# Two-block transformer kernel: MLP up products with both activation parts as one 512-column operand, scale applied after the down products, four transfers moved in the load queue

## Chip, cores and metric

The kernel runs on one core of one Trainium2 chip. The metric is the device time of one execution in microseconds. The kernel before was timed three times; the median is 1084.58 us (1083.57 to 1085.78).

## The reference, cut to what matters

A sequence of 256 tokens with 1024 channels goes through two transformer layers and then through a second block. Three MLPs of the same form lie on the way, each with 4096 hidden channels, all in float32:

```python
def rmsnorm(x, g):
    return x * rsqrt(mean(x * x, -1) + EPS) * g
def sq_relu_mlp(h, w_up, w_down):
    u = relu(h @ w_up)
    return (u * u) @ w_down
x = x + sq_relu_mlp(rmsnorm(x, g_mlp), w_up, w_down)     # MLP 0 and MLP 1, first block
x = x + square(relu(rmsnorm_2(x, g2) @ w_ff1)) @ w_ff2   # MLP 2, second block
```

Around them stand a gated linear attention, a sliding-window attention, and in the second block a mixer with an input projection of 5888 columns, a full attention of 8 heads, a dilated attention of 12 heads and gates.

## The kernel before, in words

**Products.** TensorE works on float32 values in a reduced format (fp32r). To keep precision, every operand stands as a high part (rounded to fp32r) and a low part (the rest), and a product is three matmuls: high x high, high x low, low x high (`prod`, L269). In `gemm_a` (L284) the weights are the stationary operand (128 x 128) and the transposed activations hT move, 256 columns (all tokens) per matmul, so the order of one product is weight-high with hT-high, weight-high with hT-low, weight-low with hT-high: three matmuls and three weight loads. In the down products and `gemm_b` the activations are stationary and 512 columns of weights move.

**Weights.** They come in 161 blocks of 1 MB at most (2048 floats per partition). Numbered from 0, blocks 17 to 48 are MLP 0, 58 to 89 MLP 1, 90 to 112 the second input projection (of which 105 to 108 are gate a and 109 to 112 gate b), 113 to 116 the output projection of the full attention, 117 and 118 that of the dilated one, 119 to 122 `w_out_2` ("po"), 123 to 154 MLP 2, 155 to 160 the end. A block is loaded into one of three raw buffers, ACT rounds it into one of three high buffers (`highs_to`, L1674), and DVE subtracts to get the low part (`lows_to`, L932), in two instructions of 1024 columns per block. At the start of block i (`take`), ACT makes the high part of block i+2, which waits for its transfer and for PE's last use of block i-1; DVE makes the low part of block i+1. All engines work in program order, so what stands behind such a wait waits too.

**The load queue.** All loads are issued by SyncE in one order written by hand (`sync_program`, L2252). `weights_to(n)` issues all blocks below n; block j waits for the low part of block j-3, which frees its raw buffer. Between these calls stand small loads that wait for their destination to come free, and hold up every block behind them: the two halves of the gate bias (L2315, which waits for the last transposed head to be read out, and L2317, which waits for the end of the dilated attention), the input p_2 (L2319, waits for the last head of the full attention) and the last norm's gain (L2321, waits for the transposes of p).

**An MLP** (`mlp`, L406 on PE, L1055 on DVE, L1768 on ACT) has 16 up tiles of 256 hidden channels and 16 down blocks, in eight chunks of two and two. The up tiles of chunk c+1 come before the down blocks of chunk c. An up tile is one PSUM bank: i = 0, 1 (128 channels each) times eight k, so 16 products. Four PSUM banks (4 to 7) are taken in turn for it, by the transposes and by small products; banks 0 to 3 hold the sum of the down products. When an up tile is full:

1. DVE writes r = max(tile, 0) times RB, the reciprocal root of the norm, with the row of tokens along the free dimension (L1063). RB comes from a matmul of ones with a diagonal matrix (`rows_scale`, L374 on PE, L1020 on DVE, and `diagonals`, L1013), which can only be made after the sum of squares, DVE and POOL work beside the first tiles. So tiles 0 and 1 are both read out after tile 1.
2. ACT squares r in place (L1776) and rounds it into the high part of u (L1779).
3. DVE subtracts and gets the low part of u (L1070).

At the start of an MLP the first tile is cut in two halves over k; between them PE transposes the second half of x (`norm_rest`, L367), ACT rounds it and DVE makes its low part (L1724, L985), and PE goes on. ACT's high part of the third block of the MLP stands ahead of these roundings in ACT's order. At the end DVE adds the four down sums to x (`add_x`, L1038).

The lines that decide the order of an up tile on DVE:

```python
        def fill(n):                                     # L1058
            for w in due(K.full(tile), m_free, *rb(s)):
                dve.wait_ge(*w)
            stt(r, K.bank(tile), 0.0, RB[:, :], ALU.max, ALU.mult).then_inc(*K.emptied(tile))
        def down_chunk():                                # L1086
            for kk in range(2):
                take()
                u_lows()
```

## Time and profile before

| | before |
|---|---|
| median of three runs | 1084.58 us |
| the profiled execution's own time | 1084.3 us |
| its span in the profile | 1082.5 us |
| TensorE clock granted, mean | 0.98 |
| PE matmul busy | 1023.6 us (95%) |
| weight loads busy (beside the matmuls) | 895.3 us (83%) |
| DVE busy | 647.5 us (60%) |
| ACT busy | 491.1 us (45%) |
| weights read by the load queue | 180.16 MB |

The span runs from the first to the last instruction; the time of an execution is 1.8 us longer. Busy time of PE says that the engine had a matmul under way, not that it ran at its peak: matmuls overlap, and what one costs is read from the starts of consecutive ones.

### The profile page before, as it was taken

The numbers are of one execution on the slowest core, as the hardware profiler recorded it, in microseconds if no ns is written. First come the engines' busy times: TensorE is split into PE (matmuls) and PEld (weight loads), VectorE is DVE, ScalarE is ACT, GpSimd is POOL, SyncE is SP. The second block draws the span as 40 slices with busy tenths as digits, with TensorE's granted clock in tenths as the row PEclk, the third lists the DMA queues.
The fourth block names the chain that finished last, engine by engine and source line by source line (L and its number), as shares of the span: only waits on it lengthen the run. The fifth ranks groups of instructions, "written<-read, shape, count | busy, mean of one in ns | idle before, by whom it ended". The sixth has DMA issues, their size and how long they took to land.

```text
span 1082.5 us, 14500 instructions
## 1 busy us (share of the span) xinstructions
PE 1023.6 (95%) x6158; PEld 895.3 (83%) x6158; DVE 647.5 (60%) x909; ACT 491.1 (45%) x573; POOL 43.2 (4%) x57
## 2 busy tenths in 40 slices
PE   6989999999999879999999999899999799999996
PEld 5866789999989768999989889778777699999975
DVE  4665766555456876645554756675666565455564
ACT  4353445444435654534444464243564344444452
POOL 1000100000000000000000111300000000000001
PEclk8989999999999999999999999899999899999999
DMA  7772475556653326655566465231336446646541
GB/s 216 254 242 78 152 237 195 161 190 200 213 183 106 117 78 200 229 184 161 190 202 210 133 207 182 93 122 35 141 127 214 156 132 216 197 156 194 176 165 49
DMA packets 115033, 181.09 MB, mean 167 GB/s; under 512 B 4351, under 2 KB 78567, under 8 KB 114968
## 3 DMA queue, kind: packets, MB, share of 16 engines
q1 hardware_dynamic: 114968, 180.16, 50.5%
q8 instruction: 48, 0.79, 0.3%
q14 instruction: 17, 0.14, 0.0%
HBM read 179.05 MB, written 5.55 MB: 171 GB/s over the span
## 4 chain that ended last, share of the span: by engine, by line
PE 84%; DVE 6%; DMA 4%; ACT 2%; POOL 2%; issue 1%; SPq 0%; DVEq 0%; POOLq 0%; ACTq 0%
PE ps L263 81%; PE ps L267 3%; DMA raw<-in_a_w_in 2%; DVE wlo L916 2%; DVE M L924 1%; DVE M L916 1%; POOL st L2161 1%; DMA raw<-in_w_ff 1%; ACT whi L1666 1%; ACT RR L1666 1%; DMA raw<-in_w_in 1%; POOL M L2161 0%; ACT M L1663 0%; DVE M L920 0%; DMA x<-in_x 0%
## 5 line engine op out<-in xcount | busy, mean ns | idle before, releaser
L263 PE MATMUL ps<-whi,RR 128*128 128x512 f32 (+2 forms) x1568 | 495.8, 391 | 9.4 <-DVE wlo L916 5.7
L1666 ACT ACTIVATE whi<-raw 128x2048 fp32r<-128x2048 f32 (+1 forms) x161 | 302.3, 1880 | 232.4 <-PE ps L263 201.1
L916 DVE TENSOR_TENSOR wlo<-raw,whi 128x1024 fp32r<-128x1024 f32 (+1 forms) x322 | 372.5, 1200 | 55.4 <-ACT whi L1666 55.2
L263 PE MATMUL ps<-RR,whi 128*128 128x256 f32 (+1 forms) x2016 | 371.1, 286 | 17.6 <-DVE RR L924 12.3
L263 PEld LDWEIGHTS ps<-whi,RR 128*128 128x128 f32 x1568 | 295.2, 190 | 73.8 <-issue 10.0
L263 PEld LDWEIGHTS ps<-RR,whi 128*128 128x128 f32 (+1 forms) x2016 | 318.5, 193 | 23.7 <-DVE RR L924 13.3
L263 PE MATMUL ps<-wlo,RR 128*128 128x512 f32 (+2 forms) x784 | 304.3, 388 | 0.0
L263 PE MATMUL ps<-RR,wlo 128*128 128x256 f32 (+1 forms) x1008 | 287.0, 285 | 0.0
L263 PEld LDWEIGHTS ps<-RR,wlo 128*128 128x128 f32 (+1 forms) x1008 | 194.6, 193 | 0.2
L263 PEld LDWEIGHTS ps<-wlo,RR 128*128 128x128 f32 x784 | 149.1, 190 | 27.7
L924 DVE SCALAR_TENSOR_TENSOR M<-ps,RB 128x512 f32<-128x512 f32 x52 | 35.7, 691 | 177.0 <-PE ps L263 176.2
L1663 ACT ACTIVATE M<-M 128x512 f32<-128x512 f32 (+3 forms) x58 | 41.8, 727 | 159.7 <-DVE M L924 159.4
L263 PE MATMUL ps<-M 128*64 128x128 f32 (+5 forms) x416 | 67.6, 337 | 6.1 <-ACT M L1666 3.2
L263 PEld LDWEIGHTS ps<-M 128*64 128x64 f32 (+2 forms) x416 | 47.2, 164 | 23.4 <-issue 13.5
L1666 ACT ACTIVATE M<-ps 128x512 f32<-128x512 f32 (+2 forms) x49 | 28.4, 597 | 72.9 <-PE ps L267 37.4
L2158 POOL TENSOR_SCALAR st<-st 128x2 f32<-128x2 f32 (+3 forms) x13 | 7.7, 595 | 907.8 <-DVE st L1007 640.5
L267 PE MATMUL ps<-ident,M 128*128 128x128 f32 (+1 forms) x194 | 28.5, 283 | 14.6 <-DVE M L920 6.3
L267 PEld LDWEIGHTS ps<-ident,M 128*128 128x128 f32 (+1 forms) x194 | 22.3, 144 | 22.2 <-issue 14.6
L1666 ACT ACTIVATE RR<-ps,G 128x256 fp32r<-128x256 f32 x64 | 25.1, 480 | 32.3 <-PE ps L267 32.3
L924 DVE SCALAR_TENSOR_TENSOR RR<-ps,G,RR 128x256 fp32r<-128x256 f32 x64 | 26.4, 477 | 21.0 <-ACT RR L1666 21.0
L916 DVE TENSOR_TENSOR x<-x,ps 128x512 f32<-128x512 f32 x24 | 16.5, 686 | 30.3 <-PE ps L263 30.3
L916 DVE TENSOR_TENSOR RR<-M,RR 128x512 fp32r<-128x512 f32 x48 | 32.6, 685 | 0.0
(87 smaller groups left out, 394.0 us busy)
## 6 DMA issues: line engine op xcount, KB each, us to landing
raw<-in_w_up SPq DMA_DIRECT2D x32, 1024.0 KB, 5.4
raw<-in_w_down SPq DMA_DIRECT2D x32, 1024.0 KB, 5.0
raw<-in_w_ff SPq DMA_DIRECT2D x32, 1024.0 KB, 5.4
raw<-in_w_in SPq DMA_DIRECT2D x23, 1024.0 KB, 5.3
raw<-in_a_w_in SPq DMA_DIRECT2D x12, 1024.0 KB, 7.5
raw<-in_a_w_out SPq DMA_DIRECT2D x4, 1024.0 KB, 5.3
raw<-in_b_w_q SPq DMA_DIRECT2D x4, 1024.0 KB, 5.2
raw<-in_b_w_out SPq DMA_DIRECT2D x4, 1024.0 KB, 5.0
```

The lines of the kernel that those rows point to most:

```text
L263: return pe.matmul(out, lhsT, rhs, start=start, stop=stop, skip_group_check=True)
L267: return pe.transpose(out, in_, ident[0:n, 0:n])
L916: return dve.tensor_tensor(out, a, b, op)
L924: return dve.scalar_tensor_tensor(out=out, in0=a, scalar=s, in1=b, op0=op0, op1=op1)
L1663: return act.activation(out, in_, f, **k)
L1666: return act.activation(out, in_, ACT.Copy, **k)
L2158: return pool.tensor_scalar(out, a, s1, s2, op0, op1)
L2161: return pool.tensor_tensor(out, a, b, op)
```

## The change

In the up products of the three MLPs hT's high and low parts, which lie one after the other in the same tensor, become one moving operand of 2 x 256 columns. A product is then two matmuls: weight-high with both parts (512 columns into a whole PSUM bank), and weight-low with hT-high (256 columns, added onto the second half of the bank). A tile of two such banks holds two unfinished sums side by side, and takes a pair of banks. ACT copies the second halves to SBUF, DVE adds the first halves, then DVE computes max(r, 0) * r from SBUF in one instruction; ACT rounds the result, DVE subtracts, as before. RB, the diagonal and the rows matmul are gone from the MLPs: since the square of relu(c x) is c squared times that of x, for c above 0, the square of the norm factor is applied per token (per partition) when the down sums are added to x. POOL computes it (`squared` in place of `eighth`). In the load queue the four small loads each stand two weight blocks later.

```diff
--- before.py
+++ after.py
@@ -140,6 +140,8 @@
                     RR[:, a + 2048:a + 4096].rearrange("p (k t) -> p k t", t=T))
         self.hT, self.yT = parts(0), parts(4096)
+        self.hT2 = RR[:, 0:4096].rearrange("p (a k t) -> p k a t", a=2, t=T)
         self.uT = [(RR[:, 4096 + 2048 * i:5120 + 2048 * i].rearrange("p (k t) -> p k t", t=T),
                     RR[:, 5120 + 2048 * i:6144 + 2048 * i].rearrange("p (k t) -> p k t", t=T)) for i in range(2)]
         self.oB = (RR[:, 8192:8704].rearrange("p (k t) -> p k t", t=T),
@@ -313,6 +315,36 @@
                 after(f)
             yield
+    def gemm_up(name, w, c0, n, ready, hook=None):
+        for f in range(0, n, 256):
+            j, hi, lo = block(w[:, c0 + f:c0 + f + 256], 8, 256)
+            tile = name + (f,)
+            take(tile, *misc_pair())
+            b = K.pair(tile, 512)
+            for w_ in due(K.at("w_lo", j)):
+                pe.wait_ge(*w_)
+            halves = [(0, 4), (4, 8)] if hook and f == 0 else [(0, 8)]
+            for k0, k1 in halves:
+                for i in range(2):
+                    for k in range(k0, k1):
+                        for w_ in due(ready(k)):
+                            pe.wait_ge(*w_)
+                        mm(b[:, i, :].rearrange("p (a t) -> p a t", a=2), hi[:, k, 128 * i:128 * i + 128],
+                           V.hT2[:, k, :, :], k == 0, False)
+                        t = mm(b[:, i, T:2 * T], lo[:, k, 128 * i:128 * i + 128], hT[0][:, k, :], False, k == 7)
+                    if i == 0 and len(halves) == 1:
+                        yield
+                if len(halves) == 2 and k0 == 0:
+                    at = turn["misc"]
+                    hook()
+                    turn["misc"] = at
+                    yield
+            t.then_inc(*K.filled(tile))
+            K.value["w_used", j] = K.full(tile)
+            yield
     def gemm_b(name, w, c0, n, xT, ready, pairs=None):
         kt = xT[0].shape[1]
@@ -405,16 +437,9 @@
     def mlp(l, up, down, s, after):
         ready = h_ready(s)
-        seen = {"n": 0}
-        def scaled(f):
-            seen["n"] += 1
-            if seen["n"] == 2:
-                rows_scale(s)
         def up_chunk(c4):
-            return gemm_a(("up", l, 2 * c4), up, c4 * 512, 512, hT, ready,
-                          (lambda: norm_rest(s)) if c4 == 0 else None, scaled)
+            return gemm_up(("up", l, 2 * c4), up, c4 * 512, 512, ready, (lambda: norm_rest(s)) if c4 == 0 else None)
         dn = {}
@@ -1041,6 +1066,13 @@
             dve.wait_ge(*w)
         tt(xc, xc, K.bank(tile), ALU.add).then_inc(*K.emptied(tile))
+    def add_scaled(tile, n, c, s):
+        xc = x[:, c, n * 512:n * 512 + 512]
+        for w in due(K.full(tile), K.at("rstd2", s)):
+            dve.wait_ge(*w)
+        stt(xc, K.bank(tile), st[:, 6 + c:7 + c], xc, ALU.mult, ALU.add).then_inc(*K.emptied(tile))
     def project(name, s, hook):
         g = gemm_b(D, 8, lambda f, m, c: add_x((name, f, c), f // 512, c))
         next(g)
@@ -1052,15 +1084,19 @@
-    def mlp(l, s, after, m_free):
+    def mlp(l, s, after):
         state = {"n": 0, "late": []}
         def fill(n):
             tile = ("up", l, n // 2 * 2, n % 2 * 256)
             r = V.up_r(n)
-            for w in due(K.full(tile), m_free, *rb(s)):
-                dve.wait_ge(*w)
-            stt(r, K.bank(tile), 0.0, RB[:, :], ALU.max, ALU.mult).then_inc(*K.emptied(tile))
+            r2 = r.rearrange("p (i t) -> p i t", i=2)
+            for w in due(K.at("up_low", (l, n))):
+                dve.wait_ge(*w)
+            tt(r2, r2, K.pair(tile, T), ALU.add).then_inc(*K.emptied(tile))
+            for w in due(K.empty(tile)):
+                dve.wait_ge(*w)
+            stt(r, r, 0.0, r, ALU.max, ALU.mult).then_inc(*K.up("up_u", (l, n)))
             state["late"].append(n)
         def u_lows():
@@ -1073,14 +1109,7 @@
         def evac(f):
             n = state["n"]
             state["n"] += 1
-            if n == 0:
-                diagonals(s)
-                return
-            if n == 1:
-                rows_scale(s)
-                fill(0)
-            else:
-                u_lows()
+            u_lows()
             fill(n)
         def down_chunk():
@@ -1094,7 +1123,7 @@
             for n, c in ((0, 0), (0, 1), (1, 0), (1, 1)):
                 if (n, c) == (1, 1):
                     norm_early(after)
-                add_x(("dn", l, n, c), n, c)
+                add_scaled(("dn", l, n, c), n, c, s)
         g = gemm_a(512, evac, lambda: norm_rest(s))
         next(g)
@@ -1307,7 +1336,7 @@
     gated(1)
     project("pa", 1, lambda: turn_parts("to", 1, None))
-    mlp(0, 1, 2, K.full(("to", 1, 1)))
+    mlp(0, 1, 2)
@@ -1404,7 +1433,7 @@
     next(attn)
     run_all((project_by_rows(), 1), (attn, 1))
-    mlp(1, 3, 4, K.empty(("pr", 1, 1)))
+    mlp(1, 3, 4)
@@ -1618,7 +1647,7 @@
     tt(pT[1].rearrange("p k t -> p (k t)"), K.bank(("pT",)), pT[0].rearrange("p k t -> p (k t)").bitcast(F32),
        ALU.subtract).then_inc(*K.emptied(("pT",)))
-    mlp(2, 5, 6, K.full(("ty", 1, 1)))
+    mlp(2, 5, 6)
@@ -1765,27 +1794,23 @@
-    def mlp(l, s, after, u_free):
+    def mlp(l, s, after, m_free, u_free):
         state = {"n": 0}
         def fill(n):
             tile = ("up", l, n // 2 * 2, n % 2 * 256)
             r = V.up_r(n)
-            for w in due(K.empty(tile)):
+            low = K.pair(tile, 512)[:, :, T:2 * T]
+            for w in due(K.full(tile), m_free, *([K.at("u_lo", (l, n - 4))] if n >= 4 else [])):
                 act.wait_ge(*w)
-            d = step(actf(r, r, ACT.Square))
-            for w in due(d, *(u_free if n < 4 else [K.at("u_free", (l, n // 2 - 2))])):
+            copy(r.rearrange("p (i t) -> p i t", i=2), low).then_inc(*K.up("up_low", (l, n)))
+            for w in due(K.at("up_u", (l, n)), *(u_free if n < 4 else [K.at("u_free", (l, n // 2 - 2))])):
                 act.wait_ge(*w)
             copy(V.u_part(n, 0), r).then_inc(*K.up("u_hi", (l, n)))
         def evac(f):
-            n = state["n"]
+            fill(state["n"])
             state["n"] += 1
-            if n == 0:
-                return
-            if n == 1:
-                fill(0)
-            fill(n)
         g = gemm_a(512, evac, lambda: norm_rest(s))
         next(g)
@@ -1898,7 +1923,7 @@
     run_all((gg, 1))
     project(1, lambda: turn_parts("to", 1, []))
-    mlp(0, 1, 2, all_x(K, 1))
+    mlp(0, 1, 2, K.full(("to", 1, 1)), all_x(K, 1))
@@ -1966,7 +1991,7 @@
     next(attn)
     run_all((project_by_rows(), 1), (attn, 1))
-    mlp(1, 3, 4, [K.empty(("pr", 1, 1))])
+    mlp(1, 3, 4, K.empty(("pr", 1, 1)), [K.empty(("pr", 1, 1))])
@@ -2114,7 +2139,7 @@
         act.wait_ge(*w)
     copy(oB[0].rearrange("p k t -> p (k t)"), K.bank(("pT",))).then_inc(*K.up("pT_hi"))
-    mlp(2, 5, 6, [K.empty(("po", 512, 1))])
+    mlp(2, 5, 6, K.full(("ty", 1, 1)), [K.empty(("po", 512, 1))])
@@ -2173,6 +2198,11 @@
         for w in due(K.at("rstd", s)):
             pool.wait_ge(*w)
         ts(st[:, 6:8], st[:, 4:6], 0.125, None, ALU.mult, None).then_inc(*K.up("p8", s))
+    def squared(s):
+        for w in due(K.at("rstd", s)):
+            pool.wait_ge(*w)
+        tt(st[:, 6:8], st[:, 4:6], st[:, 4:6], ALU.mult).then_inc(*K.up("rstd2", s))
     def memset(name, ap, v):
         pool.memset(ap, v).then_inc(*K.up(name))
@@ -2199,7 +2229,7 @@
         pool.wait_ge(*w)
     tt(st[:, 24:32], st[:, 16:24], S["half8"], ALU.pow).then_inc(*K.up("o_rstd"))
     rstd(1, 4).then_inc(*K.up("rstd", 1))
-    eighth(1)
+    squared(1)
     rstd(2, 4).then_inc(*K.up("rstd", 2))
     eighth(2)
     for w in due(K.dma("bc", 3)):
@@ -2213,7 +2243,7 @@
         tt(c[:, 8:12].rearrange("p (b h) -> p b h", b=2), c[:, 4:8].rearrange("p (b h) -> p b h", b=2), skb,
            ALU.add).then_inc(*K.up("sw_sink", p))
     rstd(3, 4).then_inc(*K.up("rstd", 3))
-    eighth(3)
+    squared(3)
     rstd("4a", 32).then_inc(*K.up("rstd", "4a"))
     rstd("4b", 34).then_inc(*K.up("rstd", "4b"))
     for w in due(K.at("rstd", "4b")):
@@ -2233,7 +2263,7 @@
             pool.wait_ge(*w)
         tt(X3, X3, S["cos"][:, c:c + 1, :].broadcast_to([128, 10, 128]), ALU.mult).then_inc(*K.up("ro_cos", c))
     rstd(5, 4).then_inc(*K.up("rstd", 5))
-    eighth(5)
+    squared(5)
     rstd(6, 4).then_inc(*K.up("rstd", 6))
     for c in range(2):
         for w in due(K.at("end_sq", (c, 0)), K.at("end_sq", (c, 1))):
@@ -2311,13 +2341,13 @@
     weights_to(62)
     load("bias", 1, V.BB, A["toe2"].rearrange("h p c -> p h c"), K.dma("toe2"), K.empty(("pr", 1, 1)))
     load("lnf", 0, M[:, 0:1024], spread(A["ln_final"]))
-    weights_to(107)
+    weights_to(109)
     load("bg", 0, V.BG, spread(A["b_gate_2"][:, 0:1024]), K.empty(("rt", 4)))
-    weights_to(111)
+    weights_to(113)
     load("bg", 1, V.BG2, spread(A["b_gate_2"][:, 1024:2048]), K.full(("do", 1)))
-    weights_to(115)
+    weights_to(117)
     load("p", 0, V.PT, A["p_2"][0, 0].rearrange("(c p) n -> p c n", p=128), K.full(("fv", 7)))
-    weights_to(125)
+    weights_to(127)
     load("fin", 0, M[:, 0:1024], spread(A["final_norm_g_2"]), K.full(("pT",)))
     weights_to(len(K.blocks))
     for c in range(2):
```

## Rows read from the trace of the kernel before

**Rows 1.** The page's busy times (share of the span, instructions).
```profile
PE 1023.6 (95%) x6158; PEld 895.3 (83%) x6158; DVE 647.5 (60%) x909; ACT 491.1 (45%) x573; POOL 43.2 (4%) x57
```

**Rows 2.** The chain of waits in order of time: start us, us, what.
```profile
151.66 174.50 PE ps L263 x1118
...
753.73 6.67 DMA raw<-in_w_in
...
852.69 7.80 DMA raw<-in_w_ff
...
862.33 0.83 ACT RR L1666 x2
...
864.12 176.75 PE ps L263 x1118
```

**Rows 3.** Timeline of PE: first product of an up tile, of down blocks, of the next.
```profile
205.73 0.40 PE L263 MATMUL ps<-RR,whi 128*128 128x256 f32 x2
...
217.24 0.40 PE L263 MATMUL ps<-whi,RR 128*128 128x512 f32 x1
...
228.15 0.40 PE L263 MATMUL ps<-RR,whi 128*128 128x256 f32 x2
```

**Rows 4.** Timeline of PE around the rows matmul of MLP 2.
```profile
875.05 0.28 PE L263 MATMUL ps<-RR,wlo 128*128 128x256 f32 x1
875.17 0.59 PE L263 MATMUL ps<-dg,ones 128*128 128x256 f32 x2
...
875.84 0.28 PE L263 MATMUL ps<-RR,wlo 128*128 128x256 f32 x1
```

**Rows 5.** Timeline of PE with its idle time in brackets: after norm_rest, and full attention.
```profile
426.79 0.51 PE L263 MATMUL ps<-RR,whi 128*128 128x256 f32 x2 [1.40 <-DVE RR L924]
...
764.23 0.63 PE L267 MATMUL ps<-ident,M 128*128 128x128 f32 x4 [2.17 <-DVE M L920]
...
789.46 0.66 PE L267 MATMUL ps<-ident,M 128*128 128x128 f32 x4 [0.37 <-DVE RR L916]
...
864.12 0.79 PE L263 MATMUL ps<-RR,whi 128*128 128x256 f32 x2 [8.10 <-DVE RR L924]
```

**Rows 6.** Stretches: us, busy of PE, PEld, DVE, ACT, POOL (x); granted clock, DMA share, GB/s.
```profile
205.73:217.24 11.51, 11.51 (x97) 11.51 (x96) 3.56 (x4) 4.99 (x4) 0.00 (x0) 1.00 0.39 119
...
864.12:869.20 5.08, 5.08 (x24) 5.08 (x25) 3.92 (x8) 0.80 (x2) 1.20 (x3) 0.50 0.12 48
```

**Rows 7.** Timeline of the load queue: when each load was issued.
```profile
753.34 0.34 SPq L2263 DMA_DIRECT2D M<-in_b_gate  x1
...
832.07 4.00 SPq L2273 DMA_DIRECT2D raw<-in_w_ff  x2
852.30 0.34 SPq L2263 DMA_DIRECT2D M<-in_final_norm_g  x1
```

**Rows 8.** Timeline of DVE: low parts of blocks 109, and of 122 and 123.
```profile
741.60 2.35 DVE L916 TENSOR_TENSOR wlo<-raw,whi 128x1024 fp32r<-128x1024 f32 x2
...
840.70 4.63 DVE L916 TENSOR_TENSOR wlo<-raw,whi 128x1024 fp32r<-128x1024 f32 x4
```

**Rows 9.** Timeline of DVE and ACT after an up tile in mid-MLP is full.
```profile
211.68 0.69 DVE L924 SCALAR_TENSOR_TENSOR M<-ps,RB 128x512 f32<-128x512 f32 x1 [6.82 <-PE ps L263]
212.29 2.35 DVE L916 TENSOR_TENSOR wlo<-raw,whi 128x1024 fp32r<-128x1024 f32 x2
214.56 0.68 DVE L916 TENSOR_TENSOR RR<-M,RR 128x512 fp32r<-128x512 f32 x1
...
212.41 0.64 ACT L1663 ACTIVATE M<-M 128x512 f32<-128x512 f32 x1 [4.51 <-DVE M L924]
```

**Rows 10.** Groups by form: ACT and DVE reading a whole bank or half of one.
```profile
L1666 ACT ACTIVATE M<-ps 128x512 f32<-128x512 f32 x33 | 19.8, 600 | 62.6 <-PE ps L263 35.5 <-PE ps L267 27.1
L1666 ACT ACTIVATE RR<-ps,G 128x256 fp32r<-128x256 f32 x64 | 25.1, 480 | 32.3 <-PE ps L267 32.3
L916 DVE TENSOR_TENSOR x<-x,ps 128x512 f32<-128x512 f32 x24 | 16.5, 686 | 30.3 <-PE ps L263 30.3
```


## The prediction, made before the changed kernel was run

> **What bounds the kernel now.** I read the page's busy times first: PE is under way in 95% of the span, DVE in 60%, ACT in 45%, so the question is what PE's time is made of and where it waits [rows 1]. Then the chain of waits in order of time: each MLP is one piece of PE, 174.50 us for MLP 0 (MLP 1 is the same to 0.01) and 176.75 for MLP 2, with no wait inside. Two pieces of the chain in the second block are weight transfers, 6.67 us at 753.73 and 7.80 us at 852.69 [rows 2]. Third, PE's timeline, where the starts of consecutive matmuls give the price of one [rows 3], and where the brackets give the idle time at those two places [rows 5]. Last, the load queue and the two other engines around them [rows 7 to 9].
>
> **Part 1: one weight load and one matmul less per product.** From the first up product at 205.73 to the first down product at 217.24 lie 11.51 us and two tiles, 2 x 16 products x 3 = 96 matmuls: 0.1199 us per 256 columns. From there to 228.15 lie 10.91 us and two down blocks, 48 matmuls: 0.2273 us per 512 columns [rows 3]. The clock is fully granted, which is the 2.4 GHz level [rows 6]. The second 256 columns cost 0.2273 - 0.1199 = 0.1074, so 0.1199 - 0.1074 = 0.0125 us of a matmul do not depend on its columns. The number of columns does not change (512 + 256 for 3 x 256); one such fixed share goes. The new product is 0.2273 + 0.1199 = 0.3472 for 0.3597 now. There are 3 x 16 x 16 = 768 of them: 768 x 0.0125 = **9.6 us**. It all lies on PE's uninterrupted path. No mixed sequence stands in the trace, so the bounds: nothing saved at one end (0.3597). Below 0.3472 I see nothing: the fixed share is the same behind 256 and behind 512 columns, so longer cover does not shrink it.
>
> The page "TensorE: Matmul & The Clock Gate" of the Trainium skill (section Back-to-back issue gap) gives a fully clocked matmul a fixed share of only 2.5 ns beside its columns. By that rule this part would be 1.9 us. The trace has five times as much between matmuls with a weight load each, and I go by the trace.
>
> **Part 2: the rows matmul.** The low-part matmuls of consecutive products start 0.36 apart; across the rows matmul it is 875.05 to 875.84, 0.79 [rows 4]. So it costs 0.43, three times: **1.3 us**. With it go DVE's diagonals and RB copies and the wait for the norm factor, all beside PE's work: nothing.
>
> **Part 3: the gain load (last norm) moved behind blocks 125 and 126.** Now it waits for the transposes of p until 852.30, and block 125 is issued behind it at 852.69 [rows 2, 7]. It takes 7.80 us to land; ACT's rounding of it stands ahead of the four roundings of norm_rest, which start at 862.33; PE stands idle for 8.10 us [rows 2, 5]. At the start of MLP 1 the same place costs 1.40 [rows 5]. Block 125 needs only the low part of 122, which with that of 123 takes DVE from 840.70 to 845.33, about 2.3 each [rows 8]. So after the change 125 goes out at about 843.0 and 126 at 845.3 and even at 7.8 us each they are there by 853, when ACT comes to 125. What is late next is the ordinary chain transposes, ACT, DVE, 1.40. Saved 8.10 - 1.40 = 6.7. The idle time also left PE at half the clock (0.50, the 1.2 GHz level) from 864.12 to 869.20 [rows 6]: MLP 2 takes 176.75 for 174.50, another 2.25 [rows 2]. Together **8.95 us**. The moved load itself waits for nothing that is not met by then (852.30), and block 127 behind it needs a low part that DVE makes only after that.
>
> **Part 4: the second half of the gate bias behind 111 and 112.** Block 111 is issued behind it at 753.73 and ACT's rounding of it blocks the exponentials of the second head; PE idles 2.17 [rows 2, 5, 7]. After the change block 112 can go when the low part of 109 is made (741.60 + 2.35) and 111 one block earlier [rows 8], so both are there before 752. Bounds 0 and 2.17; DVE's later heads leave 0.37 at most [rows 5], so I take **2.0 us**. The other two moves (first bias half, p_2) free blocks 107, 108, 115 and 116; PE has no idle time there that ends on a transfer: nothing. Each small load passes two weight blocks and is itself due no earlier than its own wait, so none is later by more than an issue.
>
> **Part 5: the longer way out of an up tile.** Now DVE starts when the tile is full, at 211.68: 0.69, then the low part of the next block but one, 2.35, done at 214.64 [rows 9]. It must be there when the tile under way ends, 16 x 0.3597 = 5.76 us after the last; it is there after 3.0. New order: ACT copies the second halves out of two banks (whole bank 0.60), DVE adds (0.69), DVE squares (0.69), then the low part (2.35), with four hand-overs of 0.03 (ACT starts 212.41 after DVE ends 212.37): about 4.45 [rows 9, 10]. The tile is then 16 x 0.3472 = 5.56. Behind the low part stands u's (0.68): DVE is through at 5.13. If a read out of two banks costs as much as two half banks, the copy is 0.96 and the add at most 2 x 0.48: 5.1, still in time [rows 10]. So **nothing**, with 0.45 to 1.1 us of margin. If the cover fails, PE waits at the next block. ACT has as many instructions per tile as before: its squaring (0.64) goes, the copy comes, and it waits for DVE's two in between, with its rounding of weights behind that wait; that rounding feeds a low part due a block later. The raw buffer is freed 1.5 us later per up tile, and its transfer is due two blocks after; that is covered. Banks: a tile takes the pair that was read out a tile ago. The last additions to x take a scalar more, 0.06 each, behind PE's transposes: nothing.
>
> **Sum.** 9.6 + 1.3 + 8.95 + 2.0 = 21.9. The profiled execution took 1084.3 us, 0.3 less than the median of three, so the forecast is 1084.3 - 21.9 = 1062.4, rounded **1062.5 us**.
>
> **Rivals.**
> *A, the fixed share stays.* It is a price per 256 columns streamed into PSUM and not per weight load, and the new product takes 0.3597. Against it: 512 columns pay it once in the down blocks. Time 1072.0.
> *B, most of the fixed share stays.* It is a pause that belongs to the products' change of weights and operand pattern, and longer in the mixed sequence; if four fifths of it stay, 768 x 0.0125 / 5 = 1.9 us are saved, time 1084.3 - 1.9 - 12.25 = 1070.1. Rows 3 speak against it: the share is the same in both kinds of product. The skill's rule, named in part 1, comes out at the same place.
> *C, DVE sets the pace of an up tile.* The new forms cost more than rows 10 say, the low part comes after 5.56, and PE waits at each of 48 tiles. At 0.2 us each: 9.6 us, time 1072. For it: three instructions in line where one stood, and the margin falls from 2.7 to about 1.
> *D, the transfers are not what holds MLP 2's start.* Blocks 125 and 126 would come early and something else, such as ACT's order, keep PE idle; parts 3 and 4 give half: time 1068.
> *E, slower: the moving operand in two pieces.* hT-high and hT-low of one k lie 2048 elements apart. If such an operand streams at half rate, it costs what two 256-column matmuls cost at half the clock, 2 x 5.08 / 24 = 0.423 us [rows 6]; the product is then 0.543, 768 x 0.183 = 141 us more than now, and the time 1084.3 + 141 - 12.25 = 1213. It decides from the point where the new product takes over 0.3597 + 12.25/768 = 0.3757. Against it: each piece is 256 elements in one run, as the operand is now. The page "Advanced Engine Details and Errata" of the Trainium skill (section Memory Cachelines) says of PSUM that patterns with gaps slow matmuls a lot; the output here has none, and no row shows such an operand.
>
> **How the numbers follow.** The forecast has 0.66; A 0.08, B 0.05, C 0.09, D 0.08, E 0.04. The forecast's own range is 1060 to 1066. To leave out no more than 2 in 10 the range reaches to A, B and D and to C's price at 0.2 us: 1059.5 to 1073. A measurement of this kernel tells 0.2%, about 2.2 us, from no change. All cases but E are faster by more, save a heavy C (0.45 us a tile): faster 0.94, within 0.2% 0.02, slower 0.04.
>
> **What would show it.** In the profile after: two matmuls per up product, starts 0.347 apart; 32 of them from the first up to the first down product in 11.1 us; MLPs as pieces of about 170.9 us (174.50 - 3.2 - 0.43), all three alike; idle of about 1.4 at the start of MLP 2 and full clock behind it; PE hardly idle in front of the second head's transposes; blocks 125 and 126 issued before 846; no wait of PE for a weight low part within an MLP. Wrong it would be if the starts are 0.36 apart (A), 0.357 (B), over 0.376 (E), if PE waits on wlo after up tiles (C), or if the 8 us are still there (D).

## The result, and the profile after

| | before | after |
|---|---|---|
| median | 1085.05 us (1083.57 to 1085.78) | 1066.3 us (1064.24 to 1066.96) |
| the profiled execution's own time | 1084.3 us | 1064.24 us |
| its span | 1082.5 us | 1062.4 us |
| TensorE clock granted, mean | 0.980 | 0.991 |

The ratio of the times is 0.9826 (95% interval 0.9808 to 0.9844): the change makes the kernel 1.7% faster, 18.75 us by the medians, 20.06 us between the two profiled executions. The forecast was 21.9 us. The profiled execution after is the fastest of its four, so 2.06 us of the distance between the forecast 1062.5 and the median 1066.3 lie between executions of one kernel.

The page's busy times, which answer to [rows 1]. The counts differ by 774: 768 matmuls of the products, and six of the rows matmuls, each of which stands in the trace as two (the x2 of [rows 4]).

```profile
PE 1012.1 (95%) x5384; PEld 849.5 (80%) x5384; DVE 676.2 (64%) x945; ACT 489.3 (46%) x573; POOL 42.8 (4%) x57
```

The chain of waits in order of time (start us, us, what), which answers to [rows 2]: the three MLPs, and between the last two no transfer of a weight block any more.

```profile
152.23 172.58 PE ps L265 x868
...
424.35 172.25 PE ps L265 x868
...
848.58 172.26 PE ps L265 x868
```

The timeline of PE, which answers to [rows 3]: the first product of an up tile, the first down product, the next up tile.

```profile
205.31 0.39 PE L265 MATMUL ps<-RR,whi 128*128 128x512 f32 x1
...
216.60 0.40 PE L265 MATMUL ps<-whi,RR 128*128 128x512 f32 x1
...
227.54 0.39 PE L265 MATMUL ps<-RR,whi 128*128 128x512 f32 x1
```

From 205.31 to 216.60 lie 11.29 us and 32 products: 0.3528 each, where it was 11.51 / 32 = 0.3597 and where the forecast had 0.3472. This is the first difference from the forecast. (The expectations below give 0.3531 for the same distance: they count from product to product inside such a stretch, and not to the down product behind it.)

The brackets of PE's idle time, which answer to [rows 5]: at the second head 0.27 for 2.17, at the start of MLP 2 1.40 for 8.10.

```profile
755.41 0.63 PE L269 MATMUL ps<-ident,M 128*128 128x128 f32 x4 [0.27 <-DVE M L945]
...
848.58 0.50 PE L265 MATMUL ps<-RR,whi 128*128 128x512 f32 x1 [1.40 <-DVE RR L949]
```

The load queue, which answers to [rows 7]: the bias half is issued at 746.42, four weight blocks go out from 823.27 to 836.92 (the second line), and the gain load at 843.50, behind them.

```profile
746.42 0.34 SPq L2293 DMA_DIRECT2D M<-in_b_gate  x1
...
823.27 13.65 SPq L2303 DMA_DIRECT2D raw<-in_w_ff  x4
843.50 0.34 SPq L2293 DMA_DIRECT2D M<-in_final_norm_g  x1
```

DVE and ACT after an up tile is full, which answers to [rows 9].

```profile
211.78 0.69 DVE L941 TENSOR_TENSOR M<-M,ps 128x512 f32<-128x512 f32 x1 [7.34 <-ACT M L1695]
212.51 0.69 DVE L949 SCALAR_TENSOR_TENSOR M<-M 128x512 f32<-128x512 f32 x1
213.12 2.35 DVE L941 TENSOR_TENSOR wlo<-raw,whi 128x1024 fp32r<-128x1024 f32 x2
```
```profile
211.15 0.60 ACT L1695 ACTIVATE M<-ps 128x512 f32<-128x512 f32 x1 [3.67 <-PE ps L265]
```

ACT's copy out of two banks costs the 0.60 of a whole bank. The low part is done at 213.12 + 2.35 = 215.47, 4.3 us after the copy began, and PE needs it at 216.60, for the down product above.

**Where the 20 us came from.** The span is cut at the ends of the MLPs and where PE starts again after a wait. "Rope" is the rotation of queries and keys behind the second input projection; PE starts again there at 693.96 before and at 689.25 after, behind 2.23 us of idle time in both. Two stretches, from MLP 1's end to the rope and from MLP 2's end to the end, took the same in both and are left out.

| stretch | before | after | |
|---|---|---|---|
| start to MLP 0 | 151.66 | 152.23 | +0.57 |
| MLP 0 and MLP 1, pieces of the chain | 349.0 | 344.8 | -4.2 |
| from MLP 0's end to MLP 1's start | 100.6 | 99.5 | -1.1 |
| rope to the full attention's first scores | 59.28 | 57.07 | -2.2 |
| full attention, to its output projection | 43.83 | 41.91 | -1.9 |
| output projection to MLP 2 | 67.05 | 60.35 | -6.7 |
| MLP 2, piece of the chain | 176.75 | 172.26 | -4.5 |

Two savings were not forecast: the 2.2 us behind the rope, and the 1.1 us in the first block. PE was at half the clock for part of the time at both places: behind the rope for 10.2 us before and 3.4 us after, in the first block for 3.4 us in both, from 391.5 before and from 382.0 after.

### The profile page after: what moved, and what is told of

It is laid out like the page before. It is cut to its first block, busy times and chain, and to the rows that moved or that the text cites. A ratio compares the mean times of both kernels' runs of the same rounds, so it can differ in the third digit from the quotient of the medians.

```text
span 1062.4 us, 12980 instructions
## 1 busy us (share of the span) xinstructions
PE 1012.1 (95%) x5384; PEld 849.5 (80%) x5384; DVE 676.2 (64%) x945; ACT 489.3 (46%) x573; POOL 42.8 (4%) x57
## 3 DMA queue, kind: packets, MB, share of 16 engines
HBM read 179.05 MB, written 5.55 MB: 174 GB/s over the span
## 4 chain that ended last, share of the span: by engine, by line
PE 85%; DVE 7%; ACT 2%; DMA 2%; POOL 2%; issue 1%; SPq 0%; DVEq 0%; POOLq 0%; ACTq 0%
PE ps L265 82%; PE ps L269 3%; DMA raw<-in_a_w_in 2%; DVE wlo L941 2%; DVE M L949 1%; DVE M L941 1%; POOL st L2186 1%; ACT M L1692 1%; ACT RR L1695 1%; ACT whi L1695 1%; POOL M L2186 0%; DVE M L945 0%; ACT M L1695 0%; DMA x<-in_x 0%; POOL st L2183 0%
## 5 line engine op out<-in xcount | busy, mean ns | idle before, releaser
L265 PE MATMUL ps<-RR,whi 128*128 128x512 f32 (+1 forms) x1248 | 362.8, 357 | 10.9 <-DVE RR L949 5.6
L265 PEld LDWEIGHTS ps<-RR,whi 128*128 128x128 f32 x1248 | 220.3, 190 | 50.6 <-issue 8.3
L265 PEld LDWEIGHTS ps<-RR,wlo 128*128 128x128 f32 (+1 forms) x1008 | 191.5, 190 | 0.9
L941 DVE TENSOR_TENSOR M<-M,ps 128x512 f32<-128x512 f32 x56 | 38.5, 687 | 181.7 <-ACT M L1695 173.8
L1695 ACT ACTIVATE M<-ps 128x512 f32<-128x512 f32 (+2 forms) x97 | 57.1, 597 | 173.7 <-PE ps L265 138.5
L1695 ACT ACTIVATE RR<-M 128x512 fp32r<-128x512 f32 x48 | 30.4, 633 | 71.1 <-DVE M L949 71.1
L269 PE MATMUL ps<-ident,M 128*128 128x128 f32 (+1 forms) x194 | 29.4, 290 | 13.3 <-DVE M L941 4.9
L949 DVE SCALAR_TENSOR_TENSOR M<-M 128x512 f32<-128x512 f32 (+1 forms) x49 | 34.4, 703 | 1.6
```

The source lines that it names most:

```text
L265: return pe.matmul(out, lhsT, rhs, start=start, stop=stop, skip_group_check=True)
L269: return pe.transpose(out, in_, ident[0:n, 0:n])
L941: return dve.tensor_tensor(out, a, b, op)
L949: return dve.scalar_tensor_tensor(out=out, in0=a, scalar=s, in1=b, op0=op0, op1=op1)
L1695: return act.activation(out, in_, ACT.Copy, **k)
```

## The experiments

All ran against the kernel before on the same chip: 1084.28 us there in the first batch, 1083.1 in the second, 1082.6 in the third. Ratios are to it.

| run | median us | ratio (95% interval) |
|---|---|---|
| changed kernel again | 1064.58 | 0.9810 (0.9776 to 0.9845) |
| parts side by side | 1065.62 | 0.9817 (0.9785 to 0.9849) |
| moves alone | 1071.0 | 0.9878 (0.9850 to 0.9905) |
| products alone | 1077.25 | 0.9935 (0.9903 to 0.9967) |
| three matmuls | 1067.69 | 0.9856 (0.9828 to 0.9883) |
| mirrored order | 1061.06 | 0.9779 (0.9743 to 0.9815) |
| shifted starts | 1062.48 | 0.9803 (0.9765 to 0.9841) |
| first bias half back | 1066.84 | 0.9842 (0.9814 to 0.9869) |
| mirrored order again | 1060.85 | 0.9795 (0.9765 to 0.9824) |
| changed kernel, third batch | 1064.27 | 0.9825 (0.9797 to 0.9854) |
| low weights into the first half | 1063.86 | 0.9821 (0.9792 to 0.9850) |
| longer way out | 1090.7 | 1.0073 (1.0044 to 1.0101) |

### First batch: is it the operand in two pieces, and do the two halves of the change add up?

**The changed kernel again.**

> The changed kernel as it is, once more, with a profile. Its first profile has up products 0.3531 us apart (0.3472 was forecast), except the 55 products after the start of MLP 2, which are 0.3466 apart; its four runs spread over 2.7 us. If the distance is set by the instructions alone, every stretch shows the same distance as in the first profile, 0.3531 and 0.3466 at the same places, and the time is 1064 to 1067 us. If it is a state in which PE falls when it restarts after a wait, the stretch with 0.3466 is another one here, or none, or several, and each of the three MLPs that falls in it is 1.7 us shorter (256 products of 0.0065).

1064.58 us. Behind every down block the products were 0.3528 apart again, counted to the next down product. The first stretch of an MLP, between norm_rest and the first down block, is not so steady, and with it the length of the MLP: the pieces of the chain are 172.60, 172.58 and 172.58 here, 172.58, 172.25 and 172.26 in the changed kernel's first trace. The 0.33 us are some 50 products that ran 0.0065 us closer. So the instructions alone do not set the distance in the first stretch.

**hT's high and low part side by side**, so that the 512-column operand is one run of addresses.

```diff
-        self.hT, self.yT = parts(0), parts(4096)
-        self.hT2 = RR[:, 0:4096].rearrange("p (a k t) -> p k a t", a=2, t=T)
+        self.yT = parts(4096)
+        pairs = RR[:, 0:4096].rearrange("p (k a t) -> p a k t", a=2, t=T)
+        self.hT = (pairs[:, 0], pairs[:, 1])
+        self.hT2 = RR[:, 0:4096].rearrange("p (k n) -> p k n", n=2 * T)
```

> The changed kernel with the high and low parts of hT laid side by side for each k, so that the 512-column operand is one run of 512 elements and not two runs of 256. The result is the same. Theory 1 (the break in the operand costs the missing 6 ns): products 0.347 us apart in all three MLPs, 768 x 0.006 = 4.5 us less than the changed kernel, about 1061.5 us. Theory 2 (the mixed sequence of 512 and 256 columns costs it, however the operand lies): products 0.353 apart, time as the changed kernel, 1064 to 1067 us.

Nothing changes: 1065.62 us, and the same stretch of 32 products (columns: stretch, us, busy of each engine, granted clock, DMA share, GB/s):

```profile
204.60:215.89 11.29, 11.29 (x66) 9.81 (x65) 4.25 (x5) 4.96 (x4) 0.00 (x0) 1.00 0.36 127
```

The two pieces of the operand cost nothing. Rival E is far off, and the missing time is not there.

**The moves alone** (the kernel before with its four small loads two blocks later), and **the products alone** (the changed kernel with the loads back).

```diff
-    weights_to(107)
+    weights_to(109)
...
-    weights_to(111)
+    weights_to(113)
...
-    weights_to(115)
+    weights_to(117)
...
-    weights_to(125)
+    weights_to(127)
```

> The kernel before with the four small loads two blocks later and nothing else. My steps: idle before MLP 2 from 8.10 to 1.40 us and full clock behind it, 8.95 us; idle before the second head's transposes from 2.17 to about 0.2, 2.0 us; nothing from the other two. So 1084.3 - 10.95 = 1073.4 us. Rival: the first bias half moves blocks 107 and 108 up as well, and the stage of the dilated attention gets shorter by another 1 to 2 us (in the changed kernel it was 2.1 us shorter than forecast): 1071.5 us. Second rival: that shorter stage was the phase of PE's clock only, and differs from run to run.

> The changed kernel with the four small loads where they stood before. What is left is the 512-column form, the late scale and the missing rows matmul. By the distance in the first profile, 768 x (0.3597 - 0.3528) = 5.3 us and 1.3 us for the rows matmuls: 1084.3 - 6.6 = 1077.7 us, with the 8 us of idle time before MLP 2 back. By the forecast's own term (9.6 us) 1073.4 us. If the parts overlap or share a wait, the two savings of this run and of the moves alone do not add up to that of the whole change, 18.8 us.

1071.0 and 1077.25 us: 13.3 and 7.0 us less than before, together 20.3 for the 19.7 of the whole change on that chip. The second is what its expectation worked out from the measured distance (1077.7), the first is 2.4 under its own (1073.4). The two halves add up (the 95% intervals of these savings are 3 to 4 us wide to each side), and both differ from their terms: parts 3 and 4 were 10.95 and gave 13.3, parts 1 and 2 were 10.9 and gave 7.0. The 2.4 us beyond 10.95 lie behind the rope: from there to the full attention's first scores the moves alone take 56.38 us for 59.28, and their trace has no half clock there, where the kernel before had 10.2 us of it. Of the two rivals the second, the phase of PE's clock, is borne out by the comparison of traces under "The first bias half back". In the kernel with the moves alone the idle time at the three places (PE's timeline) is

```profile
709.80 0.85 PE L267 MATMUL ps<-ident,M 128*128 128x128 f32 x6 [0.94 <-DVE M L920]
...
759.99 0.63 PE L267 MATMUL ps<-ident,M 128*128 128x128 f32 x4 [0.27 <-DVE M L920]
...
853.20 0.50 PE L263 MATMUL ps<-RR,whi 128*128 128x256 f32 x2 [1.40 <-DVE RR L924]
```

as in the changed kernel. With the products alone the chain has three transfers of weight blocks (start us, us, what), one more than the kernel before:

```profile
692.61 7.24 DMA raw<-in_w_in
...
747.64 6.93 DMA raw<-in_w_in
...
848.48 6.94 DMA raw<-in_w_ff
```

The first, at 692.61, is the block behind the first half of the gate bias, whose move the forecast had counted as nothing.

### Second batch: what sets the distance of two products, and the first bias half

The changed kernel's timeline of PE shows the distance in two forms. In most stretches it goes round in threes (the starts of the 512 columns are 0.36, 0.36, 0.34, 0.35, 0.37, 0.34 apart by the rounded times of the timeline), 0.353 in the mean:

```profile
227.88 0.40 PE L265 MATMUL ps<-RR,whi 128*128 128x512 f32 x1
228.12 0.28 PE L265 MATMUL ps<-RR,wlo 128*128 128x256 f32 x1
228.24 0.40 PE L265 MATMUL ps<-RR,whi 128*128 128x512 f32 x1
...
228.60 0.40 PE L265 MATMUL ps<-RR,whi 128*128 128x512 f32 x1
...
230.00 0.40 PE L265 MATMUL ps<-RR,whi 128*128 128x512 f32 x1
```

In the first stretches of MLP 1 and MLP 2 it is even. In MLP 2 there are 11 products in 865.76 - 861.95 = 3.81 us, 0.3464:

```profile
861.95 0.39 PE L265 MATMUL ps<-RR,whi 128*128 128x512 f32 x1
...
862.30 0.39 PE L265 MATMUL ps<-RR,whi 128*128 128x512 f32 x1
...
865.76 0.39 PE L265 MATMUL ps<-RR,whi 128*128 128x512 f32 x1
```

The even form is near the forecast's 0.3472. So the price was right for a mixed sequence at its best, and most stretches are not at their best.

**Three matmuls per product again**, all else as in the changed kernel. The second half of a bank gets its start flag while the first half's sum is open, so the first halves' sums are not the reference's; number and size of the instructions are those of a product of three, and only the time is read.

```diff
-                        mm(b[:, i, :].rearrange("p (a t) -> p a t", a=2), hi[:, k, 128 * i:128 * i + 128],
-                           V.hT2[:, k, :, :], k == 0, False)
+                        mm(b[:, i, 0:T], hi[:, k, 128 * i:128 * i + 128], hT[0][:, k, :], k == 0, False)
+                        mm(b[:, i, T:2 * T], hi[:, k, 128 * i:128 * i + 128], hT[1][:, k, :], k == 0, False)
```

> Everything else of the changed kernel is kept (the pair of banks, the new way out, the loads), only the product is three matmuls with three weight loads again, 256 columns each, the first two into the two halves of the bank. If what the change saved in PE's order of work is the second load of the high weights, a product goes back to 0.360 us and the MLPs to about 174.1 us (174.5 less the rows matmul): 768 x 0.0066 = 5.1 us over the changed kernel, 1069.5 to 1071. If the time was saved by the new banks or the new way out, it stays at 1064 to 1066. The sliding-window stage between MLP 0 and MLP 1 was 100.8 us before and 99.8 after: if its shortening comes from the order of the banks it stays 99.8 here.

All three MLPs took 174.07 us (chain) and a stretch of 32 products 11.51 us, as before the change:

```profile
227.75:239.26 11.51, 11.51 (x97) 11.51 (x96) 4.25 (x5) 4.95 (x4) 0.00 (x0) 1.00 0.36 126
```

The MLPs are 1.5 to 1.8 us longer each than in the changed kernel, 5.1 together, which is the expected size. The saving within them is the missing matmul and weight load, and not the banks or the way out. The whole time, 1067.69 us, is 2 us under the expected, and the interval of its ratio overlaps the changed kernel's, so the reading rests on the MLPs' own lengths. The stage behind MLP 0 took 102.1 us here, with two half-clock stretches in it, and so says nothing of the banks.

**The mirrored order**: for odd k the short matmul first, so that short stands beside short and long beside long.

```diff
-                        mm(b[:, i, :].rearrange("p (a t) -> p a t", a=2), hi[:, k, 128 * i:128 * i + 128],
-                           V.hT2[:, k, :, :], k == 0, False)
-                        t = mm(b[:, i, T:2 * T], lo[:, k, 128 * i:128 * i + 128], hT[0][:, k, :], False, k == 7)
+                        def low():
+                            return mm(b[:, i, T:2 * T], lo[:, k, 128 * i:128 * i + 128], hT[0][:, k, :], False, False)
+                        if k % 2:
+                            low()
+                        t = mm(b[:, i, :].rearrange("p (a t) -> p a t", a=2), hi[:, k, 128 * i:128 * i + 128],
+                               V.hT2[:, k, :, :], k == 0, k == 7)
+                        if k % 2 == 0:
+                            t = low()
```

> The same two matmuls per product, but for odd k the 256 columns of the low weights come first and the 512 of the high ones second, so that short stands next to short and long next to long (512, 256, 256, 512, 512, 256, ...). In the traces so far 512 behind 512 cost 0.2267 and 256 behind 256 0.1200, together 0.3467, while the mixed order cost 0.3531 in most stretches and 0.3466 in a few. If the extra 0.0065 us belongs to changing between lengths at every matmul, half of the changes are gone and the product takes 0.350 or less, 1061.5 to 1063.5. If it belongs to a state PE is in behind the down products, whatever the order, the product stays at 0.353 and the time at 1064.5 to 1066.

1061.06 us. The chain has the MLPs at

```profile
152.54 171.07 PE ps L265 x868
...
425.75 171.09 PE ps L265 x868
...
848.81 171.09 PE ps L265 x868
```

and a stretch of 32 products takes 11.14 us, 0.3481 each, in every stretch behind a down block:

```profile
227.18:238.32 11.14, 11.14 (x65) 9.73 (x64) 4.25 (x5) 4.96 (x4) 0.00 (x0) 1.00 0.36 129
```

Same matmuls, same weight loads, same columns: the order alone takes 1.2 to 1.5 us from each MLP. The expected 0.350 or less per product came, and the second reading, a state whatever the order, falls. The forecast's 170.9 per MLP is met to 0.2.

**Shifted starts**: one extra matmul, overwritten by the next, ahead of the first product of a chunk (in MLP 2 of both tiles of a chunk), in sizes from 16 to 256 columns.

```diff
+            c4 = name[2] // 2
+            if hook is None and c4 and (f == 0 or name[1] == 2):
+                extra = ((32, 64, 96, 128, 160, 192, 224), (0, 256, 16, 48, 80, 112, 144),
+                         (32, 64, 96, 128, 160, 192, 224))[name[1]][c4 - 1]
...
+                if extra:
+                    mm(b[:, 0, 0:extra], hi[:, 0, 0:128], hT[0][:, 0, 0:extra], True, True)
```

> A matmul whose result is overwritten is put in front of the first up product of each chunk but the first: in MLP 0 one of 32, 64, 96, 128, 160, 192 and 224 columns in chunks 1 to 7, in MLP 1 one of 0 (none), 256, 16, 48, 80, 112 and 144, in MLP 2 as in MLP 0 but ahead of both tiles of the chunk. Behind every down block the products have so far been 0.3531 us apart. If the two distances, 0.3466 and 0.3531, are set by the point of PE's rhythm at which a stretch begins, some of the sizes give 0.3466 for the whole stretch, and the same size gives the same distance in MLP 0 and MLP 2. If the start does not matter, all are 0.3531 save where chance has it. The time: 27 extra matmuls of about 0.1 us, 2 to 3 us more than 1065, less 0.21 us for each stretch of 32 products that goes over to 0.3466.

By the starts of the low weights' matmuls, the products behind down blocks were 0.3466 apart after an extra matmul of 16, 48 or 112 columns, each tried once, and 0.3531 after one of 64, 80, 96, 128 and all above. In chunk 1, where up products and not a down block stand before the extra matmul, 32 columns gave 0.3466 in MLP 0 and in both tiles of MLP 2, and none left 0.3531. The sizes tried in both MLP 0 and MLP 2 (32, and 64 to 224) did the same in the first tile of a chunk in both. In MLP 2 the second tiles, which also follow up products, were even behind 64 and 96 columns too, so what stands before the extra matmul counts as well as its size. The MLPs take 173.21, 172.59 and 173.61 us with the extra matmuls in them, 2.3 us together over the changed kernel's first trace. That the time, 1062.48 us of two executions only, is under the expected is therefore not the products' doing: this trace has the highest clock of all, 0.994, and no half clock behind the rope. Two neighbours in MLP 1, the starts behind 112 and behind 80 extra columns (PE's timeline):

```profile
541.69 0.50 PE L265 MATMUL ps<-RR,whi 128*128 128x112 f32 x2
542.03 0.28 PE L265 MATMUL ps<-RR,wlo 128*128 128x256 f32 x1
542.15 0.39 PE L265 MATMUL ps<-RR,whi 128*128 128x512 f32 x1
...
542.50 0.39 PE L265 MATMUL ps<-RR,whi 128*128 128x512 f32 x1
...
542.84 0.39 PE L265 MATMUL ps<-RR,whi 128*128 128x512 f32 x1
```
```profile
519.34 0.50 PE L265 MATMUL ps<-RR,whi 128*128 128x80 f32 x2
519.68 0.28 PE L265 MATMUL ps<-RR,wlo 128*128 128x256 f32 x1
519.80 0.40 PE L265 MATMUL ps<-RR,whi 128*128 128x512 f32 x1
...
520.15 0.40 PE L265 MATMUL ps<-RR,whi 128*128 128x512 f32 x1
...
520.51 0.40 PE L265 MATMUL ps<-RR,whi 128*128 128x512 f32 x1
```

So the alternating order has two rhythms, and between two extra matmuls or down blocks a stretch keeps the one it starts in. Which one it is depends on the start: with the start alone changed, the same products run in the one or the other. What in the engine makes the two is open.

**The first bias half back** in front of block 107, all else as changed.

```diff
-    weights_to(109)
+    weights_to(107)
     load("bg", 0, V.BG, spread(A["b_gate_2"][:, 0:1024]), K.empty(("rt", 4)))
```

> Only the load of the first half of the gate bias goes back in front of block 107. The forecast had nothing for this move. The run with all four loads back showed ACT waiting 3.96 us for a transfer there, PE idle 2.28 us instead of 0.94 in front of the transposes, and then 3.4 us at half the clock. If that is the cost of this load, the stage from the second input projection to the second head gets 1.3 us longer, and 1.7 us more where the half clock comes too: 1066.5 to 1069. If the idle time belonged to the other three moves, it stays at 1064 to 1066.

1066.84 us, in the expected range, though its interval overlaps that of the changed kernel; the reading rests on the trace. From the rope to the full attention's first scores it took 60.03 us for 57.07, 2.96 longer. In its trace (timelines of SP, ACT and PE, then a stretch) the bias waits until 694.26 and three weight blocks behind it; ACT waits 4.17 us for one of them, PE then idles 2.48 us, and the clock is at 0.50, the 1.2 GHz level, for 3.4 us:

```profile
694.26 0.34 SPq L2293 DMA_DIRECT2D M<-in_b_gate  x1
694.64 6.94 SPq L2303 DMA_DIRECT2D raw<-in_w_in  x3
```
```profile
702.24 1.91 ACT L1695 ACTIVATE whi<-raw 128x2048 fp32r<-128x2048 f32 x1 [4.17 <-DMA raw<-in_w_in]
```
```profile
706.82 1.52 PE L269 MATMUL ps<-ident,M 128*128 128x128 f32 x6 [2.48 <-DVE M L945]
```
```profile
706.40:709.80 3.40, 2.98 (x10) 2.67 (x11) 2.28 (x4) 1.43 (x3) 0.00 (x0) 0.50 0.02 6
```

In the changed kernel PE idles 0.94 at this place: 1.54 us of waiting, and about 1.7 us from the half clock (3.4 us of work at half speed), are 3.2, near the 2.96.

The same stretch in the other traces, rope to first scores, sorted by how long PE is at half clock when it starts again at the rope:

| half clock at the rope | first bias half moved | not moved |
|---|---|---|
| none | 55.8 (four traces), 56.38 (moves alone) | 58.71 (products alone) |
| 3.4 us | 56.9 to 57.1 (five traces) | 60.03 (first bias half back) |
| 10.2 us | 59.21 (mirrored order again) | 59.28 (kernel before) |

The first two rows give 2.9 to 3.1 us for the move (2.3 against the moves alone), with the second half-clock stretch in it that follows the wait (at 705.1 and at 706.4). The last row gives 0.07: these two stretches take the same time at the same clock (0.91 in the mean), with the load moved and not.

```profile
693.96:753.24 59.28, 59.19 (x308) 46.17 (x308) 37.98 (x58) 22.44 (x37) 0.00 (x0) 0.91 0.24 81
```
```profile
690.66:749.87 59.21, 59.21 (x309) 46.24 (x309) 37.99 (x58) 22.34 (x37) 0.00 (x0) 0.91 0.24 81
```

So the 2.2 us from the kernel before to the changed one are the difference between 10.2 and 3.4 us of half clock, which is 2.1 to 2.3 with the load moved in both. Whether the moves made that stretch shorter is not shown: the mirrored kernel has the moves and had 3.4 us in one trace and 10.2 in the other.

### Third batch: the mirrored order again, and the margins

> The mirrored order once more, next to the changed kernel on the same chip. In its first run every stretch of products behind down blocks had 0.3467 us, the MLPs were 170.9 us each, and the median was 1061.06 with a spread of 6 us. If the mirrored order is the cause, the MLPs are 170.9 again and the time is 3.5 to 4.5 us under the changed kernel's in the next run, less what half-clock stretches elsewhere put in. If the first run had luck with its rhythm, as single stretches of the changed kernel had, some stretches are at 0.353 again.

> The changed kernel on the same chip as the mirrored one: 1064 to 1066.5, MLPs of 172.3 to 172.6 us counted between their waits, 0.3531 per product behind every down block.

1060.85 us for 1064.27 on the same chip, 3.4 less; the MLPs were 171.09, 171.10 and 171.09 (chain), beside 172.60, 172.58 and 172.26. The intervals of the two ratios (0.9795 and 0.9825) still overlap, with single executions of the mirrored kernel from 1058.88 to 1066.73 us; the MLPs' own lengths do not: 171.07 to 171.10 in its two traces, 172.25 and more in every trace of the alternating order. The expectation has the first run's product at 0.3467 and its MLPs at 170.9; the trace shows 0.3481 and 171.07 to 171.09, in both runs.

**The low weights' product into the first half of the bank.**

```diff
-                        t = mm(b[:, i, T:2 * T], lo[:, k, 128 * i:128 * i + 128], hT[0][:, k, :], False, k == 7)
+                        t = mm(b[:, i, 0:T], lo[:, k, 128 * i:128 * i + 128], hT[0][:, k, :], False, k == 7)
```

> The order stays long, short, long, short, but the 256-column product of the low weights is added onto the first half of the bank instead of the second; the two halves are added outside as before, so the result is the same sum. If the extra 0.0065 us comes from adding onto the 256 columns that the matmul just before has written last, it goes away: 0.3467 per product, MLPs of 170.9 us, 1060 to 1062. If it is the change between lengths at every matmul, the distance stays 0.3531 behind down blocks and the time 1064 to 1066.5.

Nothing changes: three MLPs of 172.58 us and

```profile
204.80:216.09 11.29, 11.29 (x66) 9.81 (x65) 4.25 (x5) 4.95 (x4) 0.00 (x0) 1.00 0.35 124
```

Which half is added onto does not matter; with the mirrored order this leaves the alternation of lengths. The mirrored order also puts matmuls with high weights side by side, and those with low ones; against that as the cause stands the kernel before, where all 96 matmuls of a stretch, with high and with low weights, start 0.120 apart.

**A longer way out of an up tile.**

```diff
+            for _ in range(l + 1):
+                for w in due(step(stt(r, r, 0.0, r, ALU.max, ALU.max))):
+                    dve.wait_ge(*w)
             stt(r, r, 0.0, r, ALU.max, ALU.mult).then_inc(*K.up("up_u", (l, n)))
```

> DVE gets further instructions of the same form and size (about 0.69 us each, and a hand-over) between its addition and its squaring in every up tile: one in MLP 0, two in MLP 1, three in MLP 2. In the changed kernel the low part of the next block is ready at 215.47 and the tile under way ends at 216.76, a margin of 1.3 us; the forecast had put it at 0.45 to 1.1. If 1.3 is right, MLP 0 keeps its 172.4 us, MLP 1 gets longer by little (two make 1.4 to 1.5: up to 0.2 us for each of some 15 tiles, 0 to 3 us) and MLP 2 waits for DVE at nearly every tile (0.8 to 0.9 us times 15, 11 to 14 us). If the margin were 0.45, MLP 0 would already be 3 to 5 us longer, and if DVE were no limit at all within 2 us, MLP 2 would not change.

One extra instruction (MLP 0): 172.88 us for 172.58, and its chunks repeat every 22.28 us, against 22.23 in the changed kernel (227.54 - 205.31). Two (MLP 1): every 23.08. Three (MLP 2): every 24.53 us, with PE waiting before the next block:

```profile
886.09 11.39 PE ps L265 x56
910.62 11.39 PE ps L265 x56
```
```profile
904.05 0.50 PE L265 MATMUL ps<-whi,RR 128*128 128x512 f32 x1 [0.94 <-DVE wlo L941]
...
910.62 0.50 PE L265 MATMUL ps<-whi,RR 128*128 128x512 f32 x1 [0.83 <-DVE wlo L941]
```

The third costs (24.53 - 23.08) / 2 = 0.725 us per tile, all of its length; two cost (23.08 - 22.23) / 2 = 0.425. By these two the margin is 2 x 0.725 - 0.425 = 1.03 us per tile, near the 216.60 - 215.47 = 1.13 of the trace. It is under the 1.3 that the expectation took, and so both MLPs grew by more than expected: MLP 1 takes 179.05 us, 6.5 more (0 to 3 expected), and MLP 2 190.6, 18.4 more (11 to 14).

## Why the prediction was right or wrong, point by point

- **Direction and range**: right; 1066.3 us lies in 1059.5 to 1073, and just outside the forecast's own range, 1060 to 1066. Of the 3.8 us over 1062.5, 2.06 lie between the profiled execution and the median. Between the profiled executions 21.9 were forecast and 20.06 came: part 1 is 4.5 us too large, parts 2 to 4 are right, and 2.2 and 1.1 us at places with half-clock stretches, less 0.57 before MLP 0, were in no term. That the time came within 0.4% was partly luck: the unforecast 2.7 us covered more than half of the error of part 1.
- **Part 1, the product (9.6 us): the failed step is the term 768 x 0.0125.** The step said that the fixed share was "the same behind 256 and behind 512 columns", from two sequences of one length each, and noted that no mixed sequence stood in the trace. Measured was 0.3597 - 0.3528 = 0.0069 per product, 5.3 us, with 5.1 in the pieces of the chain once the rows matmul is taken off. The runs show the reason: the sum 0.2273 + 0.1199 = 0.3472 holds in some stretches of the alternating order (0.3466), and nearly when like lengths stand side by side (mirrored: 0.3481), but behind down blocks the alternating order runs at 0.3531. Neither A (nothing saved) nor B (a fifth saved) came; 0.0069 of 0.0125 is between B and the forecast. B's second half, "longer in the mixed sequence", was the right place to look, and its price was wrong.
- The rule weighed there, from "TensorE: Matmul & The Clock Gate" of the Trainium skill (section Back-to-back issue gap), would have made part 1 1.9 us. The trace does not agree with it: 5.3 us in the alternating order, 8.9 in the mirrored (768 x 0.0116). The section gives that share for an isolated matmul, though, and says of a stream of weight loads and matmuls that both set the distance, so it was not a rule for this sequence.
- **Part 2, the rows matmul (1.3 us)**: right. MLP pieces with three matmuls per product are 174.50 with it and 174.07 without, 0.43.
- **Part 3, the gain load (8.95 us)**: right in both terms. The stage before MLP 2 is 67.05 - 60.35 = 6.70 shorter, idle 1.40; with the moves alone MLP 2 is 174.50 instead of 176.75. Rival D falls.
- **Part 4, the second bias half (2.0 us)**: right, 43.83 - 41.91 = 1.92. **"The other two moves (first bias half, p_2): nothing" held only for the clock of the trace that it was read from.** The step looked for idle time of PE that ends on a transfer and found none. The wait passes from the transfer over ACT and DVE to PE, and in the kernel before PE itself was at half clock there, so that late data found it busy (its ACT timeline, and its stretch at 0.52 of the clock):

```profile
705.01 1.91 ACT L1666 ACTIVATE whi<-raw 128x2048 fp32r<-128x2048 f32 x1 [1.63 <-DMA raw<-in_w_in]
```
```profile
695.00:705.50 10.50, 10.41 (x31) 7.40 (x30) 6.95 (x12) 1.52 (x3) 0.00 (x0) 0.52 0.61 209
```

  The cover was a slow PE, which is not work but a state that comes and goes. The move is worth 0.07 us between the two traces with that half clock, and about 2.9 where it is short or missing. How often the kernel before runs in which of these is not known. That p_2's move is worth nothing was not tried by itself.
- **Part 5, DVE's longer way (nothing, margin 0.45 to 1.1)**: right. PE has no wait for a low part within an MLP, and the margin measured 1.03. Rival C falls.
- **Rival E**: falls by the run with the parts side by side. The section Memory Cachelines of "Advanced Engine Details and Errata" in the Trainium skill, named there for PSUM, had no case here: an operand in two runs of 256 columns in SBUF costs what one run of 512 does.
- **The 1.1 us between MLP 0 and MLP 1** was in no term. The stage took 100.6 us in the two traces with the old products (before, moves alone), which have a half-clock stretch of 3.4 us from about 392; 99.5 to 99.6 where that stretch came at 379 to 384, and 102.1 in the four traces that had two, one of them with three matmuls per product. The place of the half clock goes with the length; whether the new products shift it is open.

## What to carry to other kernels

Take the price of a matmul in a new sequence from a row with that sequence; where there is none, give the mixed sequence a bound of its own, and if long and short matmuls must alternate, write them mirrored (long, short, short, long), which gave 3.4 us more here at no cost. Before a late transfer is costed at nothing, follow its wait through every engine behind it, and ask whether what covers it is work or only an engine at half clock. Before a stretch that got shorter is put down to the change, compare it between traces with the same half clock in it. A margin on a helper engine is measured best by putting known instructions into its line until the bound engine waits.

## What the runs showed of the hardware that was not expected

- Two steady rhythms for one and the same alternating sequence of 512 and 256 columns, 0.3466 and 0.3531 us per pair, kept for whole stretches and set by how the stretch begins: behind down products a single overwritten matmul of 16, 48 or 112 columns moved it to the faster one, and 64, 80, 96 and 128 or more did not; behind up products 32, 64 and 96 did.
- Half-clock stretches of 3.4, 6.8 or 10.2 us come in different places from execution to execution of one kernel: the mirrored kernel's two traces have spans of 1061.6 and 1064.9 us at mean granted clocks of 0.988 and 0.982, with the same MLPs to 0.02 us. Where PE starts again after 2.2 us of idle time ahead of the rope (689.25 in the changed kernel), the clock was at 0.50 for 3.4 us in the first trace of the changed kernel, for 10.2 us in the second of the mirrored one, and full in the changed kernel's second trace; the stretch to the first scores took 57.07, 59.21 and 55.78 us accordingly. What a removed wait gives back depends on that.
